# A gated linear recurrence: its smallest score level from the log decays, its query scaling at half width, and its decayed keys and queries made one stage earlier

## What is computed

```python
def chunk_step(S, xs):
    q_c, k_c, v_c, lf_c = xs
    cum = jnp.cumsum(lf_c, axis=2)
    rel = jnp.where(causal[:, :, None], cum[:, :, :, None, :] - cum[:, :, None, :, :], -jnp.inf)
    attn = jnp.einsum('bhtd,bhsd,bhtsd->bhts', q_c, k_c, jnp.exp(rel))
    o = attn @ v_c + jnp.einsum('bhtd,bhde->bhte', q_c * jnp.exp(cum), S)
    last = cum[:, :, -1:, :]
    S = (jnp.exp(last[:, :, 0, :, None]) * S
         + jnp.einsum('bhsd,bhse->bhde', k_c * jnp.exp(last - cum), v_c))
    return S, o
```

## Time and profile before

| | us |
|---|---|
| median of three executions | 2433.7 |
| lowest and highest of them | 2428.29, 2438.26 |
| the profiled execution's own time | 2435.62 |
| its span in the profile | 2433.8 |
| mean granted TensorE clock, share of full | 0.957 |
| TensorE matmul, busy | 2124.1 (87%) |
| VectorE, busy | 1440.0 (59%) |
| ScalarE, busy | 609.1 (25%) |
| GpSimd, busy | 460.1 (19%) |

### The profile page before, as it was taken

The page is one execution under the profiler, slowest core; times in us unless marked ns, Lnnn a source line. Parts: engine busy times, 40 slices in busy tenths (PEclk is TensorE's granted clock), DMA queues, the critical chain, the costliest instruction groups (busy, mean ns, idle before and its releaser), DMA issues. The chain is left out here.

```text
span 2433.8 us, 28142 instructions
## 1 busy us (share of the span) xinstructions
PE 2124.1 (87%) x10768; PEld 1433.4 (59%) x10768; DVE 1440.0 (59%) x2441; ACT 609.1 (25%) x1005; POOL 460.1 (19%) x400
## 2 busy tenths in 40 slices
PE   7788898987997777777788888999998967899998
PEld 6678897774542222222267785666767855566584
DVE  5355563557888887565573565433756586433394
ACT  1311102422111111000111222333741151233372
POOL 1032100204443433333212001000101031000000
PEclk9789999999999999999998799999999988899999
DMA  5820554529999999999847002899994522489997
GB/s 198 299 105 1 200 202 158 207 95 399 389 421 421 421 421 421 422 422 419 342 168 223 1 1 81 358 355 354 396 379 173 202 75 71 161 342 354 354 407 280
DMA packets 142432, 650.99 MB, mean 267 GB/s; under 512 B 17975, under 2 KB 22735, under 8 KB 97083
## 3 DMA queue, kind: packets, MB, share of 16 engines
q1 hardware_dynamic: 94012, 354.09, 38.5%
q0 software_dynamic: 46336, 291.93, 29.4%
q10 hardware_dynamic: 1952, 3.18, 0.4%
HBM read 642.46 MB, written 16.85 MB: 271 GB/s over the span
## 5 line engine op out<-in xcount | busy, mean ns | idle before, releaser
L1827 PE MATMUL psum<-peer_uv_rows,peer_weight_diagonal 128*128 128x512 f32 x932 | 453.5, 615 | 109.5 <-DVE peer_weight_diagonal L1953 109.0
L1827 PEld LDWEIGHTS psum<-peer_uv_rows,peer_weight_diagonal 128*128 128x128 f32 x932 | 161.7, 190 | 392.1 <-DVE peer_weight_diagonal L1953 266.7
L1960 DVE SCALAR_TENSOR_TENSOR peer_uv_rows<-peer_uv_rows,peer_x 128x1024 f32<-128x1024 f32 x233 | 285.6, 1226 | 144.8 <-DMA peer_uv_rows<-peer_uv,peer_index 142.5
L1781 POOL DMA_INDIRECT peer_uv_rows<-peer_uv,peer_index x233 | 242.3, 1040 | 452.8 <-PE psum L1827 333.7
L147 DVE TENSOR_TENSOR moe_weight_parts<-weight_ring,moe_weight_parts 128x2048 fp32r<-128x2048 f32 x80 | 182.6, 2291 | 155.9 <-ACT moe_weight_parts L2844 155.4
L1860 ACT ACTIVATE peer_gelu<-peer_dots 128x1 f32<-128x1 f32 x256 | 51.5, 202 | 549.8 <-DVE peer_uv_rows L1960 499.0
L2844 ACT ACTIVATE moe_weight_parts<-weight_ring 128x2048 fp32r<-128x2048 f32 x80 | 152.1, 1911 | 39.3 <-DMA weight_ring<-moe_w 26.4
L153 PE MATMUL psum<-moe_weight_parts,moe_block_x_parts 128*128 128x512 f32 x352 | 143.6, 408 | 11.6 <-DVE moe_block_x_parts L147 7.1
L155 PE MATMUL psum<-moe_weight_parts,moe_block_x_parts 128*128 128x512 f32 x352 | 140.5, 399 | 0.0
L154 PE MATMUL psum<-moe_weight_parts,moe_block_x_parts 128*128 128x512 f32 x352 | 140.4, 399 | 0.0
L2963 POOL DMA_INDIRECT h_t<-moe_tokens,moe_block_tokens x30 | 36.9, 1231 | 505.5 <-PE psum L2662 412.5
(11 more groups left out here) (577 smaller groups left out, 4074.5 us busy)
## 6 DMA issues: line engine op xcount, KB each, us to landing
weight_ring<-moe_w SPq DMA_DIRECT2D x76, 2048.0 KB, 10.4
weight_ring<-ada_w SPq DMA_DIRECT2D x24, 2048.0 KB, 9.4
moe_weight_ring_end<-moe_w SPq DMA_DIRECT2D x20, 2048.0 KB, 12.5
weight_ring<-w_in SPq DMA_DIRECT2D x17, 2048.0 KB, 9.3
weight_ring<-hgrn_w_in SPq DMA_DIRECT2D x8, 2048.0 KB, 9.8
moe_results<-moe_block_out POOLq DMA_DIRECT2D x26, 512.0 KB, 10.5
weight_ring<-nsa_w_in SPq DMA_DIRECT2D x5, 2048.0 KB, 7.9
weight_ring<-peer_wq SPq DMA_DIRECT2D x4, 2048.0 KB, 7.9
```

The costliest lines, as they stand in the source:

```text
L1781: nc.gpsimd.indirect_dma_start(buffer(t), None, S.dram["peer_uv"], bass.IndirectOffsetOnAxis(ap=experts[:, t:t + 1], axis=0)).then_inc(row ...
L1827: last = nc.tensor.matmul(S.ps[:, 2 * a + c, :], diag[:, t % 4, :], v_rows(t)[:, c * BANK:(c + 1) * BANK], start=(i == 0), stop=(i == PICK ...
L1960: nc.vector.scalar_tensor_tensor(u_rows(t), u_rows(t), 1.0, x2[:, t // PICKS, :], ALU.mult, ALU.mult, accum_out=dots[:, t:t + 1]).then_inc ...
```

## The change

In the scores:

- Level 0 has blocks of two tokens, and the difference of sums at its upper token is that token's log decay. So there is no subtract(0) and no Abs: ScalarE takes Exp of the upper columns of the log decays (`lt`, the tile in `room[1]`), every second column, 1024 in all. The key's factor at level 0 is one, so GpSimd's level-0 product goes, and round 1 of TensorE reads `kT`.
- At levels 0 and 1 the queries are scaled at their upper halves alone (1024 columns in place of 2048), as at the other levels. GpSimd no longer waits for the query product there.
- VectorE's order starts with subtract(1) and then goes by level. `subtract(2)` writes the tile of the log decays and waits for the first Exp. The tiles of `fs` are other ones of the same rooms.
- GpSimd first subtracts for kd, and behind its last level multiplies kd and qe. ScalarE takes their exponentials behind its last level.

In the outputs: subtract, exponentials and products are gone, and TensorE's transposes wait for nothing but the stage's start. `w`, which holds kd, qe and the state, is allocated before the scores. In the merge stage `da_share` is gone: the product overwrites its slice of the gates.

```diff
-        share = st.sb("da_share", [P, 2, 512])
...
-                    link(nc.vector.tensor_tensor(share[:, c, :], S.ps[:, i % RING, :], gates[:, a, D + c * 512:D + (c + 1) * 512], ALU.mult))
+                    share = gates[:, a, D + c * 512:D + (c + 1) * 512]
+                    link(nc.vector.tensor_tensor(share, S.ps[:, i % RING, :], share, ALU.mult))
                     dve.wait_ge(summed, 2 * a + c + 1)
-                    nc.vector.tensor_tensor(merged[:, a, part], merged[:, a, part], share[:, c, :], ALU.add).then_inc(summed, 1)
+                    nc.vector.tensor_tensor(merged[:, a, part], merged[:, a, part], share, ALU.add).then_inc(summed, 1)
...
-def hgrn_scores(S, qT, kT, cum, at, fs, qs):
+def hgrn_scores(S, qT, kT, cum, at, lt, fs, qs, w1, w2):
...
+        ended, begun = st.sem("decays_to_end"), st.sem("decays_from_begin")
+        kd, qe = (x.rearrange("p (h t) -> p h t", h=HH) for x in (w1, w2))
...
                 def subtract(n):
                     b = 1 << n
-                    if n >= 3:
+                    if n == 2:
+                        dve.wait_ge(exped, 1)
+                    elif n >= 3:
                         dve.wait_ge(made, 4 * (n - 1))
...
-                subtract(0)
                 subtract(1)
-                keep(0)
                 for n in range(LEVELS):
                     dve.wait_ge(exped, n + 1)
                     if n >= 2:
                         dve.wait_ge(made, 4 * n)
-                    if n < 2:
-                        nc.vector.tensor_tensor(flat(qs[n % 2]), flat(qT), flat(fs[n % 3]), ALU.mult).then_inc(q_scaled, 1)
-                    else:
-                        nc.vector.tensor_tensor(half(qs[n % 2], n, 1), half(qT, n, 1), half(fs[n % 3], n, 1), ALU.mult).then_inc(q_scaled, 1)
+                    nc.vector.tensor_tensor(half(qs[n % 2], n, 1), half(qT, n, 1), half(fs[n % 3], n, 1), ALU.mult).then_inc(q_scaled, 1)
                     if n + 2 < LEVELS:
                         subtract(n + 2)
-                    if n:
-                        keep(n)
+                    keep(n)
                 keep(LEVELS)
 
             @block.scalar
             def _(act):
-                for n in range(LEVELS):
-                    act.wait_ge(subbed, n + 1)
+                act.activation(half(fs[0], 0, 1), half(lt, 0, 1), ACT.Exp).then_inc(exped, 1)
+                for n in range(1, LEVELS):
+                    act.wait_ge(subbed, n)
                     act.activation(flat(fs[n % 3]), flat(fs[n % 3]), ACT.Abs).then_inc(absed, 1)
-                    act.wait_ge(absed, n + 1)
+                    act.wait_ge(absed, n)
                     act.activation(flat(fs[n % 3]), flat(fs[n % 3]), ACT.Exp, scale=-1.0).then_inc(exped, 1)
+                act.activation(qe, cum[:, :, P:T], ACT.Exp).then_inc(begun, 1)
+                act.wait_ge(ended, 1)
+                act.activation(kd, kd, ACT.Exp).then_inc(ended, 1)
 
             @block.gpsimd
             def _(pool):
-                for n in range(LEVELS):
+                nc.gpsimd.tensor_tensor(kd, cum[:, :, P - 1:P].to_broadcast([P, HH, P]), cum[:, :, 0:P], ALU.subtract).then_inc(ended, 1)
+                for n in range(1, LEVELS):
                     pool.wait_ge(exped, n + 1)
-                    if n < 2:
-                        pool.wait_ge(q_scaled, n + 1)
                     nc.gpsimd.tensor_tensor(half(fs[n % 3], n, 0), half(kT, n, 0), half(fs[n % 3], n, 0), ALU.mult).then_inc(k_scaled, 1)
+                pool.wait_ge(ended, 2)
+                nc.gpsimd.tensor_tensor(kd, kd, kT[:, :, 0:P], ALU.mult).then_inc(ended, 1)
+                pool.wait_ge(begun, 1)
+                nc.gpsimd.tensor_tensor(qe, qe, qT[:, :, P:T], ALU.mult).then_inc(begun, 1)
 
             @block.tensor
             def _(pe):
                 for n in range(LEVELS + 1):
                     if n:
                         pe.wait_ge(q_scaled, n)
-                        pe.wait_ge(k_scaled, n)
-                    q, k = (qT, kT) if n == 0 else (qs[(n - 1) % 2], fs[(n - 1) % 3])
+                    if n >= 2:
+                        pe.wait_ge(k_scaled, n - 1)
+                    q, k = (qT if n == 0 else qs[(n - 1) % 2]), (kT if n <= 1 else fs[(n - 1) % 3])
...
-def hgrn_outputs(S, qT, kT, cum, at, v, o, w1, w2, w3):
+def hgrn_outputs(S, at, v, o, w1, w2, w3):
...
-                nc.vector.tensor_tensor(kd, cum[:, :, P - 1:P].to_broadcast([P, HH, P]), cum[:, :, 0:P], ALU.subtract).then_inc(subbed, 1)
-                dve.wait_ge(exped, 2)
-                nc.vector.tensor_tensor(kd, kd, kT[:, :, 0:P], ALU.mult).then_inc(scaled, 1)
-                nc.vector.tensor_tensor(qe, qe, qT[:, :, P:T], ALU.mult).then_inc(scaled, 1)
                 dve.wait_ge(turned, 2)
...
-            @block.scalar
-            def _(act):
-                act.activation(qe, cum[:, :, P:T], ACT.Exp).then_inc(exped, 1)
-                act.wait_ge(subbed, 1)
-                act.activation(kd, kd, ACT.Exp).then_inc(exped, 1)
-
             @block.tensor
             def _(pe):
-                pe.wait_ge(scaled, 1)
...
-            hgrn_scores(S, qT, kT, cum, at, (room[0], room[1], room[3]), (room[2], S.hT))
+            hgrn_scores(S, qT, kT, cum, at, room[1], (room[0], room[3], room[1]), (room[2], S.hT), w[:, 0, :], w[:, 1, :])
```

More of the change, by code:

```diff
@@ L3387, in _ @@
                         last.then_inc(made, 1)
-def hgrn_outputs(S, qT, kT, cum, at, v, o, w1, w2, w3):
+def hgrn_outputs(S, at, v, o, w1, w2, w3):
     nc = S.nc
     with Stage(S, "outputs") as st:
-        subbed, exped, scaled, turned, moved, stated, state_moved, made, out_moved, chain = (st.sem(n) for n in (
-            "subtracted", "exped", "scaled", "turned", "moved", "stated", "state_moved", "made", "out_moved", "chain"))
+        turned, stated, state_moved, made, out_moved, chain = (st.sem(n) for n in (
+            "turned", "stated", "state_moved", "made", "out_moved", "chain"))
         view = lambda x: x.rearrange("p (h t) -> p h t", h=HH)
@@ L3475, in run_hgrn @@
         project(S, S.hT, units, on_act, on_dve)
-        kT, cum, at = sb("k_t"), sb("cum"), sb("scores_t")
+        kT, cum, at, w = sb("k_t"), sb("cum"), sb("scores_t"), sb("w", (P, 3, D))
         with ExitStack() as inner:
@@ L3479, in run_hgrn @@
             hgrn_decays(S, f, room[1], room[2], kT, cum)
-            hgrn_scores(S, qT, kT, cum, at, (room[0], room[1], room[3]), (room[2], S.hT))
-        with nc.sbuf_tensor("hgrn_o", [P, NT, HH, P], F32) as o, nc.sbuf_tensor("hgrn_w", [P, 3, D], F32) as w:
-            hgrn_outputs(S, qT, kT, cum, at, v, o, w[:, 0, :], w[:, 1, :], w[:, 2, :])
+            hgrn_scores(S, qT, kT, cum, at, room[1], (room[0], room[3], room[1]), (room[2], S.hT), w[:, 0, :], w[:, 1, :])
+        with nc.sbuf_tensor("hgrn_o", [P, NT, HH, P], F32) as o:
+            hgrn_outputs(S, at, v, o, w[:, 0, :], w[:, 1, :], w[:, 2, :])
             head_norm_gate_turn(S, o, g[:, :, :].rearrange("p a (h d) -> p (a h) d", d=P), S.dram["hgrn_out_gain_2"], HH, S.hT, extra=ada_slots(3, 3, 4, 5))
```

## The result

The changed kernel takes 2417.8 us (median of ten executions, 2412.3 to 2424.1) against 2433.8 for the kernel before (ten, 2428.3 to 2438.3). The ratio is 0.9939 with a 95% interval of 0.9927 to 0.9951: 14.8 us less, 11.9 to 17.8. Forecast were 2417.4 and 16.3 less.

What follows compares the result with a forecast made beforehand. A string of stages with barriers between, each ended by its last engine, VectorE gapless through most of the scores. 10.4 - 0.2 + 3.4 + 2.7 = 16.3 us off 2433.7 gave 2417.4 us; range 2410 to 2427.

Steps and rivals of the forecast that it cites:

- The outputs stage: Subtract, exponential and product leave the path, 3.4 us saved; transposes and state matmuls at clock 1.00 save 2.7 us.
- Rival C: Outputs stage: TensorE's clock falls all the same, 2417.4 + 2.7 = 2420.1 us; chance 0.12.
- The start: Start of the scores, ahead of level 1's keep: 13.76 us in place of 24.16, 10.4 us saved.
- the sum of 11.40: Start of the scores: VectorE's remaining instructions ahead of level 1's keep, 11.40 us before adding 2.36 for kd's subtraction.
- rival D: Scores: GpSimd's key products fall on VectorE's half products instead of under the keeps, 19.3 us longer, 2436.7; chance 0.03.
- The end of the scores: GpSimd's two added products end after VectorE's last keep; 0.2 us charged for what sticks out.
- the 5.12 of the pair: End of the scores: length in us charged for GpSimd's two added products, ending at 2014.51.
- Rival B: End of the scores: GpSimd's products are on the path, last keep slips 2.56 or 5.12 us, 2420.0 or 2422.5; chance 0.12.
- Levels 1 to 6: Scores: same instructions, order and buffers, VectorE without a gap, so 29.9 us stay.
- The merge stage: Four 0.68 us products write over the gates instead of their own tile; same count and length, cost 0.
- rival E: Behind the two stages: the time is given back, as if a transfer bounded the rest, 2433.7 us; chance 0.05.
- Rival A: Start of the scores: the first hold costs nothing, kd's subtraction lands under keep(0), 2415.0 us; chance 0.10.

Runs made afterwards that it cites:

- kd_on_scalar: The changed kernel with GpSimd's subtraction for kd removed; ScalarE takes Exp(last - cum) head by head behind its last level: 2418.5 us, ratio 0.9934.
- scalar_and_k2: The changed kernel with the edits of kd_on_scalar and k2_behind_subtract together: 2417.1 us, ratio 0.9929.
- k2_behind_subtract: The changed kernel with GpSimd's key product of level 2 also waiting until VectorE's subtract(3) is done: 2417.1 us, ratio 0.9935.
- filled_idle: The changed kernel with unread matmuls of constants in TensorE's idle time of the scores and after the transposes: 2415.4 us, ratio 0.9923.
- outputs_only: The kernel before with the changed outputs stage, kd and qe made in the scores, levels 0 and 1 as before: 2429.9 us, ratio 0.9992.
- share_back: The changed kernel with the da_share tile back in the merge stage: one execution, 2415.5 us.

## Why the prediction was right, and where its steps failed

**The outputs stage** came out as reasoned. The removed path was 3.59 us against 3.4; the barrier takes 0.79 from last work to first, I had 1.0 from the barrier before. The clock gave 2.66 against 2.7. Rival C, the clock falling all the same, didn't happen here, but it isn't refuted: in kd_on_scalar and scalar_and_k2, whose idle ahead of the transposes is hardly longer (1.9 against 1.55 us), the clock fell a little later and 1.5 to 1.6 us were lost. k2_behind_subtract had the same 1.9 us and lost nothing (outputs 11.84), so the length of this idle alone doesn't decide it. What does is open.

**The start** was overrated by 2.4 us, in three pieces (of start-to-start times): one that cost less than charged and two that had no term. The hold by kd's subtraction was 1.7, less than the charged 2.36: that subtraction is 1.89 long on GpSimd, shorter than any GpSimd product in the rows of before. The step that failed is that the sum of 11.40 had nothing for GpSimd's key products of levels 1 and 2. I had written that the Abs and Exp pair "is done before its product is due". It is, but I didn't follow what its end sets off. That of level 1 runs until 1.15 us after VectorE asks for its half product (1.04 lost), and that of level 2 is asked for 0.10 us ahead of subtract(3) (2.16 lost). Together that makes 2.6 us more than the sum; the other steps came out 0.15 shorter than charged. The second is rival D's mechanism. I had priced it for all levels or none; it struck once. It mended itself, as the rival's counter-argument said: from level 3 on Exp again ends 0.4 to 0.5 us after the subtraction has started. The prediction's own signs show the miss. The first stretch of VectorE is 16.20 us, over the 16 that was named as a sign of being wrong; the scores stage is 47.26 us long and not 43.6 to 44; subtract(3) was to start without a wait. The holds of 1.73 and 2.17 were each taken out by an experiment; that of level 1 is read from the rows alone, and at least 0.8 of it stayed in every version.

**The end of the scores** was to cost 0.2, because GpSimd would stick out. It ended 1.54 us ahead of the last keep instead (0.4 where no round was slow), so the 5.12 of the pair was a poor price: the long one in it is the level-1 product, which takes 2.84 alone, while qe's takes 2.38 and kd's 3.37 with a wait for VectorE's half product of 1.42 in it. Rival B didn't happen; VectorE's last half product got its turn (1.42). The 1.19 us that were lost there have a cause I had looked for in the outputs only: one round at the low clock. I had taken the 2 us gaps as harmless, from stretches that read 1.00. filled_idle shows that they aren't: with the gaps filled no round falls. Before, the rounds at the end all took 3.84 us, so the slow one in the changed order was a cost that no row at the end of the stage showed.

**Levels 1 to 6** kept their 29.9 us wherever no late round was slow (29.85 to 30.0 in six of the eight experiments and in before; the other two, outputs_only and share_back, are at 31.0). **The merge stage** is 0, and **what lies behind** took 401.38 us before and 400.95 after. In the ten profiles that part varies from 396.27 to 401.62, so they show only that nothing larger was given back; that something of the gain arrived is shown by the ratio, at least 11.9 us less, which rules rival E out. Rival A (a free first hold) was wrong by the 1.73 us that kd_on_scalar took out.

**The number.** The forecast of 2417.4 is 0.4 from the median, but its sum of 16.3 is 3.3 above what the stages show, so that closeness is in part luck. The rest lies within the interval of the ratio (11.9 to 17.8 saved) and no run separates it from the spread of executions. The direction, the places and the terms of the outputs were argued rightly; the term of the start was 2.4 too large on 8.0.

## What to carry to other kernels

When an edit shortens one engine's list, redo the time table of the engine that it can't run beside, request by request. VectorE and GpSimd, when both read two operands from SBUF, kept each other out for a whole instruction here, so 0.1 us decided over 2. A wait that puts the slower engine's request behind a short step of the faster one can save time. A stage that is bound by another engine can still be lengthened at its end by TensorE's clock, and cheap matmuls into a bank that is about to be overwritten took that away here.

## What was unexpected of the hardware

- The granted clock fell to 0.5 inside a group of matmuls, after gaps of only 2.0 us between groups of 3.8; in the changed order in the same rounds in two profiles, in other orders in other rounds. In the one profile of filled_idle, with 1.3 us of such a gap filled, it read 1.00 for 58 us.
- On GpSimd a product of 1024 columns in runs of two took 2.84 to 2.85 us, in longer runs 2.36 to 2.40, and the subtraction with one operand repeated along the columns 1.89.
- Where the requests of the changed order came at the same distances, the held instructions were as long to 0.02 us in every kernel: 4.02 and 4.03 for the first subtraction, 2.23 and 2.24 for the half product of level 1, or 1.98 to 2.00 without kd's subtraction. The holds could be removed one by one and added up: 16.20 - 1.73 - 2.17 = 12.30, measured 12.31.
